# Small sum products written one after the other into one group of rows, in place of four groups side by side

## The reference, cut to what matters

```python
# rwkv7_time_mix, H = 16 heads of N = 64
kk = heads(k * k_k)
kk = kk / jnp.maximum(jnp.sqrt(jnp.sum(kk * kk, axis=-1, keepdims=True)), 1e-12)
# mamba2_ssd_mix, 8 groups of 256 channels
y = rms_norm(y.reshape(bsz, seq, MB_GROUPS, -1), norm_g.reshape(MB_GROUPS, -1))
# swa_sink_attention, 16 query and 4 key heads of 64
q = rms_norm(q.reshape(bsz, seq, Hq, Dh), q_norm)
k = rms_norm(k.reshape(bsz, seq, Hk, Dh), k_norm)
```

## Time and profile before

| | |
|---|---|
| median of 3 runs | 3245.42 us (3240.4 to 3245.76) |
| the profiled execution | 3245.42 us, span 3243.7 us |
| mean granted TensorE clock | 0.962 |
| TensorE busy | 3103.4 us, 96% of the span |
| VectorE, ScalarE busy | 2365.1 us (73%), 1399.6 us (43%) |

### The profile page before, as it was taken

How to read it: one execution, slowest core, us unless ns; L and a number is a source line. 1 busy time by engine, 2 the same in 40 slices (tenths; PEclk the granted TensorE clock), 3 DMA queues, 4 the chain that set the end, 5 groups by cost and what they waited for, 6 DMA issues and landing times.

```text
span 3243.7 us, 49952 instructions
## 1 busy us (share of the span) xinstructions
PE 3103.4 (96%) x19946; PEld 2721.7 (84%) x19946; DVE 2365.1 (73%) x3491; ACT 1399.6 (43%) x2222; POOL 97.0 (3%) x187
## 2 busy tenths in 40 slices
PE   7998988999999999999999999999989999999998
PEld 6886678888889888888896888887688888889887
DVE  5978864788886875888867888877652776765685
ACT  3534121454544663545444544533111544465453
POOL 0000000000000000000000000000000000000000
PEclk9998997999999999999999999999988999999899
DMA  8774421567675435675664666662200553444453
GB/s 323 260 283 146 164 94 59 202 243 276 243 273 208 152 117 212 233 290 207 258 240 155 246 257 236 230 222 98 111 1 3 212 189 130 164 162 147 151 190 130
DMA packets 69671, 609.49 MB, mean 188 GB/s; under 512 B 7728, under 2 KB 7888, under 8 KB 31824
## 3 DMA queue, kind: packets, MB, share of 16 engines
q1 hardware_dynamic: 42768, 459.41, 37.9%
q0 software_dynamic: 26352, 144.88, 11.9%
q10 hardware_dynamic: 336, 2.13, 0.2%
HBM read 604.30 MB, written 2.10 MB: 187 GB/s over the span
## 4 chain that ended last, share of the span: by engine, by line
PE 86%; DVE 9%; ACT 2%; issue 2%; DMA 1%; SPq 0%; DVEq 0%; POOLq 0%; ACTq 0%
PE psum L312 28%; PE psum L884 23%; PE psum L888 12%; PE psum L905 10%; PE psum L912 6%; PE psum L310 4%; PE psum L909 1%; PE psum L1630 1%; DMA weights<-in_weights 1%; DVE arena L772 1%; DVE ada_sum L494 1%; PE psum L1579 1%; DVE arena L2214 1%; DVE wkv_base L1980 0%; DVE small L1979 0%
## 5 line engine op out<-in xcount | busy, mean ns | idle before, releaser
L835 ACT ACTIVATE unit_high<-weights 128x1024 fp32r<-128x1024 f32 x594 | 628.5, 1060 | 706.8 <-PE psum L888 388.5
L841 DVE TENSOR_TENSOR unit_low<-weights,unit_high 128x1024 fp32r<-128x1024 f32 x594 | 725.4, 1223 | 199.3 <-ACT unit_high L835 198.9
L884 PE MATMUL psum<-h_part,unit_high 128*128 128x512 f32 x3168 | 823.3, 397 | 20.5 <-DVE h_part L759 14.1
L884 PEld LDWEIGHTS psum<-h_part,unit_high 128*128 128x128 f32 x3168 | 578.1, 191 | 128.9 <-issue 16.7
L888 PEld LDWEIGHTS psum<-h_part,unit_low 128*128 128x128 f32 x3168 | 447.0, 193 | 29.5
L888 PE MATMUL psum<-h_part,unit_low 128*128 128x256 f32 x3168 | 468.1, 284 | 0.0
L312 PE MATMUL psum<-in_part,w_part 128*128 128x256 f32 x2784 | 361.4, 290 | 7.8 <-issue 4.7
L312 PEld LDWEIGHTS psum<-in_part,w_part 128*128 128x128 f32 x2784 | 348.5, 196 | 23.6 <-issue 11.3
L905 PE MATMUL psum<-hidden,unit_high 128*128 128x512 f32 x1386 | 354.0, 397 | 0.0
L1011 DVE TENSOR_REDUCE arena<-psum 128x256 f32<-128x512 f32 x396 | 272.4, 688 | 60.3 <-PE psum L888 48.6
L312 PE MATMUL psum<-arena 64*128 64x128 f32 (+7 forms) x2304 | 275.0, 294 | 26.7 <-DVE arena L2065 9.1
(11 more groups left out here) (308 smaller groups left out, 2790.7 us busy)
## 6 DMA issues: line engine op xcount, KB each, us to landing
weights<-in_weights SPq DMA_DIRECT2D x290, 1536.0 KB, 6.5
ada_in<-in_ada_w POOLq DMA_DIRECT2D x182, 768.0 KB, 5.9
consts<-in_consts POOLq DMA_DIRECT2D x1, 1700.0 KB, 14.7
x<-in_x SPq DMA_DIRECT2D x1, 1024.0 KB, 8.8
v_first<-arena ACTq DMA_DIRECT2D x1, 1024.0 KB, 3.9
arena<-v_first ACTq DMA_DIRECT2D x1, 1024.0 KB, 4.8
weights<-in_weights SPq DMA_DIRECT2D x1, 512.0 KB, 7.1
out<-x SPq DMA_DIRECT2D x1, 512.0 KB, 2.6
```

The costliest lines, as they stand in the source:

```text
L835: k.nc.scalar.activation(k.unit_part[0][:, n % UNIT_RING], w, ACT.Copy).then_inc(k.sem["unit_high"], 1)
L841: k.nc.vector.tensor_tensor(k.unit_part[1][:, n % UNIT_RING], w, k.unit_part[0][:, n % UNIT_RING].bitcast(FP32), ALU.subtract).then_inc(k. ...
L884: mm(k.psum[:, 2 * (j % 2) + half, :].rearrange("p (i t) -> p i t", i=2), lhsT=part(2 * j + half, 0, t), rhs=k.h_parts[:, :, t], start=t = ...
```

## The change

The packed sums become single products. Each tile's squares have a product of their own, and all of them accumulate into the same few rows at the lowest partitions: 16 rows in RWKV, 4 in Mamba (for each half), 24 in attention. In RWKV they stand behind k tiles 1 to 7 and in the middle of r tile 0 (`key_sum`), in attention behind tiles 2 to 11 (`head_sums(0)` to `head_sums(9)`) and two among the values; in Mamba they keep their places. Root, reciprocal and spread work on 16, 4 and 24 partitions in place of 128. One constant is 8 columns narrower.

```diff
@@ head_group_sums @@
-def head_group_sums(k, pr, r, src, first, last, signal):
-    for g in range(4):
-        pr.mm(k.psum[32 * g:32 * g + 32, 3, 0:T], k.const("head_rows")[:, 22 - 2 * r:54 - 2 * r], src[:, 4 * r + g],
-              first, last, signal if last and g == 3 else None)
@@ RwTiles @@
-        self.norm = k.rms
-        self.norm_rows = cut(26, 1024)
+        self.norm = k.rms[0:16, :]
+        self.norm_rows = cut(26, 1024)[0:16]
@@ rw_products @@
-    def key_sums(r):
-        if r == 0:
+    def key_sum(t):
+        if t == 0:
             pe.wait_ge(s["mod_ready"], n + 2 if early_mod(n) else n + 1)
-        evacuated("k", 4 * r + 3)
-        head_group_sums(k, pr, r, z.squares, r == 0, r == 1, s["rw_key_sums"])
+        evacuated("k", t)
+        mm(k.psum[0:16, 3, 0:T], k.const("head_rows")[:, 22 - 2 * t:38 - 2 * t], z.squares[:, t], t == 0,
+           t == KT - 1, s["rw_key_sums"] if t == KT - 1 else None)
@@ beside_k, beside_r @@
-        if half and m == 4:
-            key_sums(0)
+        if half and m:
+            key_sum(m - 1)
...
         if at == (0, 0):
-            key_sums(1)
+            key_sum(KT - 1)
@@ rw_act @@
-    picks = k.const("ident").rearrange("p (g n) -> p g n", g=4)
-    rows = z.norm_rows.rearrange("p (r g h c) -> p r g h c", r=2, g=4, h=2)
-    for r in range(2):
-        act_(rows[:, r], picks[:, :, 2 * r:2 * r + 2].unsqueeze(3).to_broadcast([P, 4, 2, 64]), f.Copy)
+    act_(z.norm_rows.rearrange("p (n c) -> p n c", n=16), k.const("ident", 16)[:, 0:16].unsqueeze(2).to_broadcast([16, 16, 64]),
+         f.Copy)
@@ rw_vector @@
-    v.tensor_scalar(z.norm, k.psum[:, 3, 0:T], 1e-24, None, ALU.max).then_inc(s["rw_norm"], 1)
+    v.tensor_scalar(z.norm, k.psum[0:16, 3, 0:T], 1e-24, None, ALU.max).then_inc(s["rw_norm"], 1)
@@ mb_products, group_sums and spread @@
-        for r in range(2):
-            for g in range(4):
-                mm(k.psum[32 * g:32 * g + 32, 7, T:2 * T], k.const("ones")[:, 0:32], z.sq[:, 2 * g + r], r == 0, r == 1,
-                   s["mb_group_sum"] if r and g == 3 else None)
+        for t in range(8):
+            mm(k.psum[0:4, 7, T:2 * T], k.const("pick")[:, 23 - t // 2:27 - t // 2], z.sq[:, t], t == 0, t == 7,
+               s["mb_group_sum"] if t == 7 else None)
...
-            at = 32 * (2 * (pair % 2) + n)
-            mm(k.psum[:, bank, n * T:(n + 1) * T], k.const("ident")[:, at:at + 1].to_broadcast([P, P]),
-               z.rms, True, True, s["mb_spread"] if n else None)
+            row = 2 * (pair % 2) + n
+            mm(k.psum[:, bank, n * T:(n + 1) * T], k.const("ident", 4)[:, row:row + 1].to_broadcast([4, P]),
+               z.rms[0:4], True, True, s["mb_spread"] if n else None)
@@ sw_products, head_sums and spread @@
-    def head_sums(r):
-        pe.wait_ge(s["sw_squares"], 4 * r + 4)
-        head_group_sums(k, pr, r, z.sq, r == 0, r == 2, s["sw_head_sum"])
+    def head_sums(t):
+        pe.wait_ge(s["sw_squares"], t + 1)
+        mm(k.psum[0:24, 3, 0:T], k.const("head_rows")[:, 22 - 2 * t:46 - 2 * t], z.sq[:, t], t == 0, t == 11,
+           s["sw_head_sum"] if t == 11 else None)
...
-                at = 32 * g + 2 * r + half
                 mm(k.psum[64 * half:64 * half + 64, bank, n * T:(n + 1) * T],
-                   k.const("ident")[:, at:at + 1].to_broadcast([P, 64]), z.rstd, True, True,
+                   k.const("ident", 24)[:, 2 * t + half:2 * t + half + 1].to_broadcast([24, 64]), z.rstd, True, True,
                    s["sw_spread"] if n and half else None)
...
-        if m in (5, 9):
-            head_sums(m // 4 - 1)
+        if m >= 2:
+            head_sums(m - 2)
...
     values_of(range(2))
-    head_sums(2)
+    head_sums(10)
+    head_sums(11)
     values_of(range(2, 5))
```

More of the change, by code:

```diff
@@ L215, in const_parts @@
     parts["pick"] = pick
-    head_rows = np.zeros((P, 54))
+    head_rows = np.zeros((P, 46))
     head_rows[:64, 22] = head_rows[64:, 23] = 1
@@ L2266, in __init__ @@
         self.bt = cut(14.75, 128)
-        self.acum, self.dt, self.dtx, self.e32, self.z32, self.z32b, self.da = \
-            (cut(25 + 0.25 * i, T, 32) for i in range(7))
-        self.rms = cut(26.75, T)
+        self.acum, self.dt, self.dtx, self.e32, self.z32, self.z32b, self.da, self.rms = \
+            (cut(25 + 0.25 * i, T, 32) for i in range(8))
         self.cols = k.small[:, 128:256].rearrange("p (w b h) -> p w b h", w=2, b=2)
@@ L2455, in root @@
         act.wait_ge(s["mb_group_sum"], half + 1)
-        act_(z.rms, k.psum[:, 7, T:2 * T], f.Sqrt, bias=k.const("eps"), scale=1.0 / 256)\
+        act_(z.rms[0:4], k.psum[0:4, 7, T:2 * T], f.Sqrt, bias=k.const("eps", 4), scale=1.0 / 256)\
             .then_inc(s["mb_rms"], 1)
@@ L2563, in inverse @@
         dve.wait_ge(s["mb_rms"], half + 1)
-        v.reciprocal(z.rms, z.rms).then_inc(s["mb_rstd"], 1)
+        v.reciprocal(z.rms[0:4], z.rms[0:4]).then_inc(s["mb_rstd"], 1)
     def normed(pair, bank):
@@ L2654, in __init__ @@
         self.pt = [cut(11.75 + 0.375 * i, 384) for i in range(2)]
-        self.rstd = cut(12.5, T)
+        self.rstd = cut(12.5, T, 24)
         self.stat = [k.small[:, 256 + 8 * i:264 + 8 * i] for i in range(3)]
@@ L2691, in spread @@
         for n, (which, m) in enumerate(SW_SPREADS[i]):
-            r, g = divmod(KT * which + m, 4)
+            t = KT * which + m
             for half in range(2):
-                at = 32 * g + 2 * r + half
                 mm(k.psum[64 * half:64 * half + 64, bank, n * T:(n + 1) * T],
-                   k.const("ident")[:, at:at + 1].to_broadcast([P, 64]), z.rstd, True, True,
+                   k.const("ident", 24)[:, 2 * t + half:2 * t + half + 1].to_broadcast([24, 64]), z.rstd, True, True,
                    s["sw_spread"] if n and half else None)
@@ L2782, in sw_act @@
     act.wait_ge(s["sw_head_sum"], 1)
-    act_(z.rstd, k.psum[:, 3, 0:T], f.Sqrt, bias=k.const("eps"), scale=1.0 / 64).then_inc(s["sw_rms"], 1)
+    act_(z.rstd, k.psum[0:24, 3, 0:T], f.Sqrt, bias=k.const("eps", 24), scale=1.0 / 64).then_inc(s["sw_rms"], 1)
     def exponentials(i):
```

## The result

The changed kernel takes 3270.14 us (median of 4 runs, 3265.6 to 3283.17), the kernel before 3245.59 us beside it (3240.4 to 3248.51): a ratio of 1.008, 95% interval 1.0062 to 1.0098. It is slower, as forecast, but by 24.5 us (20 to 32 by the interval) and not by 16.8, which is above the stated range of 3254 to 3268. The profiled execution took 3266.77 us with a span of 3264.3.

The account below looks back on a forecast made before the run. TensorE, busy 96% of the span and carrying 86% of the chain, was taken as the bound. RWKV 5.2, Mamba 5.3 and attention 6.3 us sum to 16.8, so 3245.4 becomes 3262 us (+0.5%), range 3254 to 3268.

Parts of the forecast that it names:

- the Mamba delay: First Mamba half: eight single sums delay ScalarE's root by 2.57 us, passing through to VectorE, which leads the chain.
- the stalls: TensorE's idle times of 4.52 and 2.93 us in the RWKV mixers absorb +1.29 us each, leaving about 3.2 and 1.6.
- A narrow single: One scattered narrow sum on TensorE costs 0.55 us from its start to the next form's; 0.74 in attention.
- the rival of no change of form: Outputs under 32 columns run in full mode at 0.43 us each, 10.6 us in all: 3256 us; chance 9%.
- The part ahead of the last w2/a2 product: RWKV mixers: sums of tiles t = 0 to 4 add +2.38 us each mixer, on the chain.
- The sum at full clock: Whole kernel: RWKV 5.2, Mamba 5.3 and attention 6.3 us add 16.8 us, giving 3262 us.
- The spread keeps its two 64-column halves and its count; only the rows shrink to 24: Attention spread: same passes with fewer rows, so no cost was added for it.
- the 16-row spread: RWKV norm spread behind the stall: 16-row weights in place of 128 cost one more change of form, +0.2 us.
- a stretch that might go away when a stall shrinks: First RWKV mixer: the low-clock stretch behind the 4.52 us stall goes, giving back 2.2 us: 3260; chance 23%.
- Unpaired 24-row spreads: Attention: 24-row, 64-column spread passes might not run in pairs, +5 us, 3267; within the more-than-the-sum rival, 11%.
- Hidden: Sums are swallowed by waits in the first Mamba half and most of the attention stream: about 3251 us; chance 6%.
- The faster case: Filled small idle times keep stretches at 2.4 GHz, 2.2 us back each; ten would give 3240 us; chance 4%.

Follow-up runs that it names:

- e2: The changed kernel with its narrow sums, but spreads over 128 rows (first and last sum product 128 columns wide): 3262.24 us, ratio 1.0058 to the kernel before.
- e12: The changed kernel run once more, unchanged, beside the kernel before: 3268.59 us, ratio 1.0081.
- e3: The changed kernel with every single sum product 128 columns wide and all spreads over 128 rows: 3248.43 us, ratio 1.0023 to the kernel before.
- e4: e3 with the change's spreads over 16, 4 and 24 rows: 3266.35 us, ratio 1.0081 to the kernel before.
- e10: e3 with all spreads over 64 rows in place of 128: 3266.39 us, ratio 1.008 to the kernel before.
- e11: e3 with all spreads over 72 rows in place of 128: 3262.29 us, ratio 1.0058 to the kernel before.
- e6: e3 with only the attention spread over 24 rows: 3259.26 us, ratio 1.0056 to the kernel before.
- e7: e3 with only the spreads of the two RWKV mixers over 16 rows: 3263.33 us, ratio 1.0065 to the kernel before.
- e8: e3 with only the Mamba spreads over 4 rows: 3257.03 us, ratio 1.0045 to the kernel before.
- e9: The kernel before with packed sums gathered further, both RWKV rounds at r0, all three attention rounds among the values: 3240.92 us, ratio 1.0007.

## Why the prediction missed

**The sign and the path were right.** TensorE was the bound, and what was added to its queue was paid. The chain is the same, the Mamba delay went through ScalarE to VectorE (3.33 - 0.82 = 2.5 us, 2.57 foretold), and the stalls swallowed what they were to swallow: 3.27 and 1.69 us left, 3.2 and 1.6 foretold.

**The prices were right.** A narrow single was put at 0.55 us and took 0.53; in attention 0.74 and 0.73; eight in Mamba 3.57 and 3.55. That 16, 4 or 24 columns pay as 32 do holds, so the rival of no change of form falls. The rule of the Trainium skill ("TensorEngine Tiling (Array Packing)", Key Properties) that a mode change drains TensorE agrees once more: the 128-column single, in the form of its neighbours, was 0.32 us cheaper. The part ahead of the last w2/a2 product came out as 1.8 us and not 2.4 in the first mixer; its clock was 0.95 in place of 0.93, which is about 1 us less at 1.2 GHz and, at half speed, 0.5 us of work, so some 2.3 at one clock. In attention the piece grew by 7.83 us and not by 6.3; the eight passes of 3.59 us at 1.2 GHz account for 3.59 - 1.99 = 1.6 of that (the same eight took 1.99 before), and 6.2 is left.

**The sum at full clock was right within the error.** e2 has the change's narrow sums at level low time, and 18.8 us (12.6 to 25.3). For the changed kernel, low time above before's is 266 - 243 = 23 us in the first comparison (266 being the mean over its 14 runs, before's 243 that of the first session) and 263 - 244 = 19 in e12; at 0.35 these are 7 to 8 us. 16.8 + 8 = 25, measured 24.5. The slope comes from runs of one kernel and is carried over, so this is an estimate that fits, with some 6 us of error on either side. e3, at the no-change-of-form price, was 10.6 by the rival's sum and came out at 7.5, with 12 us less low time than before, which are 4 us: 11.7.

**What failed** is the step "The spread keeps its two 64-column halves and its count; only the rows shrink to 24", and its like for RWKV, where the 16-row spread was charged +0.2 for a change of form. The rows were costed at nothing, because the passes last as long. They do: 2.81 us for 24 in both kernels. What they change is the clock at and behind them: 7 to 8 us in all, by the low time, and 8 us by the medians of the changed kernel and of e2, which has its sums and 128-row spreads (3270 and 3262). The granted clock was in the prediction only as a stretch that might go away when a stall shrinks (23%), or as a gain (4%); that the edit could bring new stretches was named as a way to be wrong, but had no term. The first stall did shrink to 3.27 us, and its stretch stayed (5.58 us for 16 passes in place of 5.93).

**The other rivals.** Unpaired 24-row spreads fall (2.81 us). Hidden falls. The faster case falls by sign, though its mechanism, many clock stretches, was the one that decided, the other way round.

**What stays open.** Why few rows go with more time at 1.2 GHz is not shown, only that they do, with everything else on TensorE's queue alike (e3 against e4, e10, e11). How it goes with the number of rows isn't shown either, since the start stretch may make up to 14 us of the low time of these three. The roots, clamps and reciprocals shrink with the rows in e4; in e10 and e11 only the RWKV clamp and what follows it does, to 64 and 72 partitions, which no run separates from the spreads. The parts don't add up neatly: by their medians e6, e7 and e8 are slower than e3 by 11, 15 and 9 us, 34 in all before rounding, and e4, which has all three edits, by 18. Each of these has an error of some 4 us, and e3 may have been measured a little low; the low times (23, 17 and 22, 62 in all, against 33 to 47) don't add up either. And 64 rows left the attention window at full clock (1.00) and 72 rows at before's 0.94, but neither did so in RWKV: for attention only 24 rows are shown to bring the stretch.

No version here beats the kernel before: e9 is the same, and all others are slower.

## What to carry to other kernels

Packing small products into TensorE's column groups pays only while they follow each other. Scattered, each pays the change of form on both sides, and a full-width product is then the cheaper one. When an edit shrinks the rows that a product contracts over, its own time doesn't change, but the clock behind it can: compare the mean granted clock over many runs and the windows behind the edited products, and keep zero rows in the contraction if they are free (with them the changed kernel's median was 8 us lower, e2). One trace's low-clock stretch is no proof; its return at the same place in a second trace, and the mean over a dozen runs, are.

## What the runs showed of the hardware beyond that

- Rows in use: with the same passes on TensorE, the ratio to the kernel before was 1.0023 with spreads over 128 rows, 1.0058 with 72, 1.008 with 64 and 1.0081 with 16, 4 and 24. The recorded mean time at 1.2 GHz was 231, 252, 268 and 278 us, the last three with up to 14 us of the start in them.
- The profile can give a clock of 1.00 ahead of its first change where the passes ran at half of it: 32 passes took 6.99 us at 16 us in e3 and 3.63 later in e8.
- 1 us more at 1.2 GHz went with some 0.35 us more time (0.27 to 0.41) from run to run of one kernel, not 0.5, although TensorE leads the chain for 86%.
- A contraction over 72 rows left without a change of form, one over 64 rows with it: 6.99 and 7.12 us for the same 16 passes at a clock of 0.50, 0.427 and 0.560 us from the last of them to the next full pass.
- A 128-column product between full tiles is cheaper than a 24-column one by 0.32 us.
